# A two-block transformer kernel on one core: steps at the first block's end, at the start and around the GELUs in another order

## What is computed

```python
# first block, one layer
proj   = x @ w_in                               # q, k, v of three attentions, three gates
merged = sum(sigmoid(gate_i) * (attention_i @ w_branch_i) for i in range(3))
x      = layer_norm(ALPHA * x + merged @ w_out)
hidden = silu(x @ w_ffn_in[:, :2816]) * (x @ w_ffn_in[:, 2816:])
x      = layer_norm(ALPHA * x + hidden @ w_ffn_out)
# second block, one layer
q, k, v, u, vv = split(rms_norm(x) @ w_in_2)
attn   = attention(rope(rms_norm(q)), rope(rms_norm(k)), v)
sg     = gelu(u) * (sg_w @ rms_norm(gelu(vv)) + sg_b)      # the gated branch
x      = x + concat(rms_norm(attn), rms_norm(sg)) @ w_o_2
x      = x + (silu(conv(gate)) * conv(up)) @ w_down_2      # rms_norm and w_up_2 before the conv
```

## Time and profile before

| | |
|---|---|
| time before, median of 3 runs | 1495.82 us (1495.65 to 1495.94) |
| the profiled execution's own time | 1495.67 us |
| its span in the profile | 1494.2 us |
| PE busy | 1465.1 us, 98% of the span |
| DVE busy | 1003.1 us, 67% |
| ACT busy | 784.9 us, 53% |
| POOL busy | 64.1 us, 4% |
| chain that ended last | PE 82%, DVE 10%, ACT 4%, issue 2% |
| granted TensorE clock | 1.0 over the whole span |

### The profile page before, as it was taken

The page is one execution under the profiler, slowest core; times in us unless marked ns, Lnnn a source line. Parts: engine busy times, 40 slices in busy tenths (PEclk is TensorE's granted clock), DMA queues, the critical chain, the costliest instruction groups (busy, mean ns, idle before and its releaser), DMA issues.

```text
span 1494.2 us, 18393 instructions
## 1 busy us (share of the span) xinstructions
PE 1465.1 (98%) x7191; PEld 1203.8 (81%) x7191; DVE 1003.1 (67%) x1349; ACT 784.9 (53%) x1124; POOL 64.1 (4%) x100
## 2 busy tenths in 40 slices
PE   7999999999999999999999999999999999999998
PEld 5788887888887787887878887788888888888887
DVE  5656885864556655885865555877766668777765
ACT  3565644443443555745344333686655557756553
POOL 2000000000001000000010000210000012000000
PEclk9999999999999999999999999999999999999999
DMA  8544643575564535552765664436555644455551
GB/s 317 188 155 131 237 170 124 171 241 182 184 209 156 203 116 158 183 169 85 234 214 174 201 190 169 142 115 195 184 182 169 197 151 158 155 166 187 170 188 66
DMA packets 167317, 260.99 MB, mean 175 GB/s; under 512 B 8768, under 2 KB 106720, under 8 KB 166720
## 3 DMA queue, kind: packets, MB, share of 16 engines
q1 hardware_dynamic: 166048, 252.03, 51.6%
q0 software_dynamic: 896, 6.74, 1.2%
q10 hardware_dynamic: 288, 1.05, 0.2%
HBM read 258.74 MB, written 1.05 MB: 174 GB/s over the span
## 4 chain that ended last, share of the span: by engine, by line
PE 82%; DVE 10%; ACT 4%; issue 2%; POOL 1%; DMA 1%; SPq 0%; DVEq 0%; ACTq 0%
PE ps L384 15%; PE ps L388 15%; PE ps L386 15%; PE ps L457 10%; PE ps L459 9%; PE ps L458 9%; DVE wlo L1500 3%; ACT whi L1069 2%; PE ps L1001 1%; PE ps L511 1%; PE ps L534 1%; PE ps L414 1%; DVE x L1519 1%; DVE x L1517 1%; PE ps L524 1%
## 5 line engine op out<-in xcount | busy, mean ns | idle before, releaser
L1500 DVE TENSOR_TENSOR wlo<-raw,whi 128x2048 fp32r<-128x2048 f32 (+1 forms) x238 | 528.2, 2229 | 275.0 <-ACT whi L1069 274.4
L1069 ACT ACTIVATE whi<-raw 128x2048 fp32r<-128x2048 f32 (+1 forms) x238 | 441.7, 1865 | 204.7 <-PE ps L388 124.9
L384 PE MATMUL ps<-whi,xTh 128*128 128x512 f32 x704 | 277.4, 394 | 0.0
L388 PE MATMUL ps<-whi,xTl 128*128 128x512 f32 x704 | 274.4, 390 | 0.0
L386 PE MATMUL ps<-wlo,xTh 128*128 128x512 f32 x704 | 274.1, 389 | 0.0
L457 PE MATMUL ps<-whi,xTh 128*128 128x512 f32 (+3 forms) x640 | 251.1, 392 | 7.4 <-DVE xTl L1538 3.4
L459 PE MATMUL ps<-whi,xTl 128*128 128x512 f32 (+3 forms) x640 | 242.1, 378 | 0.0
L458 PE MATMUL ps<-wlo,xTh 128*128 128x512 f32 (+3 forms) x640 | 241.4, 377 | 0.0
L388 PEld LDWEIGHTS ps<-whi,xTl 128*128 128x128 f32 x704 | 132.1, 188 | 27.9
L384 PEld LDWEIGHTS ps<-whi,xTh 128*128 128x128 f32 x704 | 132.2, 188 | 27.6 <-issue 0.8
L386 PEld LDWEIGHTS ps<-wlo,xTh 128*128 128x128 f32 x704 | 132.3, 188 | 26.4
(11 more groups left out here) (185 smaller groups left out, 1635.2 us busy)
## 6 DMA issues: line engine op xcount, KB each, us to landing
raw<-in_w_in SPq DMA_DIRECT2D x124, 512.0 KB, 4.6
raw<-in_w_ffn_in SPq DMA_DIRECT2D x88, 512.0 KB, 4.8
raw<-in_w_up SPq DMA_DIRECT2D x88, 512.0 KB, 4.9
raw<-in_w_ffn_out SPq DMA_DIRECT2D x44, 512.0 KB, 4.4
raw<-in_w_down SPq DMA_DIRECT2D x44, 512.0 KB, 4.6
raw<-in_w_branch SPq DMA_DIRECT2D x24, 512.0 KB, 4.6
raw<-in_w_out SPq DMA_DIRECT2D x16, 512.0 KB, 4.5
raw<-in_w_o SPq DMA_DIRECT2D x16, 512.0 KB, 4.5
```

What stands on the lines that cost most here:

```text
L384: PE.matmul(o, ah, hi[:, j, b], start=first and kt == 0, stop=False)
L388: mm = PE.matmul(o, al, hi[:, j, b], start=False, stop=last and j == c - 1 and i == len(kts) - 1)
L1069: AC.activation(m.whi[:, i % SPLIT, 0:w], m.raw[:, slot, 0:w], ACT.Copy).then_inc(s.w_hi, 1)
L1500: DV.tensor_tensor(m.wlo[:, i % SPLIT, 0:w], m.raw[:, slot, 0:w], m.whi[:, i % SPLIT, 0:w].bitcast(F32), ALU.subtract).then_inc(s.w_lo, 1)
```

## The change

1. Start: half 0 of x is loaded in two parts, the second on ACT's queue ahead of the layer norm's two vectors; x's half 1 is loaded behind the second weight piece instead of between the two.
2. End of the first block, both layers, on DVE: `add_down(0)` and `stats(0)` go ahead of the subtraction of piece `later`; centring and scaling are separate steps, with `hidden_half(1)` between them; the split of the second quarter and of one more weight piece go ahead of `add_down(1)`. (`later` is the number of the next layer's first piece.)
3. There on PE: the first quarter of x is transposed ahead of the last `down` step's products, not in their middle.
4. Second block: DVE counts up after each of a quarter's four remainders, and PE waits per 128 columns (`remainders=4`). At the end of its first layer the second quarter of x is transposed behind the last products. `conv_turn` stands one column block later (three matmuls).
5. First attention: in group 4, ACT's rounding of one piece goes behind both copies of transposed weights.
6. Gated branch: the one-element GELU is gone, and the GELUs of `u` stand behind group 2's exponentials, not ahead of them.

```diff
@@ sync_program
-    SP.dma_start(m.x[:, 0, :], t["x"][0, 0:P, :]).then_inc(s.x_in, 16)
+    SP.dma_start(m.x[:, 0, 0:512], t["x"][0, 0:P, 0:512]).then_inc(s.x_in, 16)
...
         load_piece(w1[:, 0:4, 0:512], 4, 512)
+        load_piece(w1[:, 4:8, 0:512], 4, 512)
         if not L:
             SP.dma_start(m.x[:, 1, :], t["x"][0, P:S, :]).then_inc(s.x_in2, 16)
-        load_piece(w1[:, 4:8, 0:512], 4, 512)
@@ tensor_program
     def x_ready(th, kt):
-        if kt in (0, 4):
-            PE.wait_ge(s.turn_lo, x_lo[th, kt // 4])
+        count, remainders = x_lo[th, kt // 4]
+        if remainders == 4:
+            PE.wait_ge(s.turn_lo, count - 3 + kt % 4)
+        elif kt in (0, 4):
+            PE.wait_ge(s.turn_lo, count)
...
         def first_x_turn(th, kt):
-            if kt == 1:
-                turn_x(0, 0)
+            if kt == 0:
+                turn_x(0, 0, remainders=last_use)
...
         def down_turn(th, kt):
             if kt == 1:
-                for n4 in range(2):
-                    turn_x(0, n4)
+                turn_x(0, 0, remainders=4)
...
         def first_conv_turn(th, kt):
-            if (th, kt) == (0, 2):
+            if (th, kt) == (0, 3):
                 bank_free(2)
                 conv_turn()
...
+        if L + 1 < DEPTH:
+            turn_x(0, 1, remainders=4)
@@ scalar_program
+    AC.dma_start(m.x[:, 0, 512:D], t["x"][0, 0:P, 512:D]).then_inc(s.x_in1, 16)
     AC.dma_start(m.vec[:, 0:D], t["ln_g"][0:1, :].broadcast_to([P, D])).then_inc(s.vec, 16)
...
-            catch(1, L, "na", g, 2, ahead=SPLIT - (g == 4))
+            catch(1, L, "na", g, 2, ahead=0 if g == 4 else SPLIT)
...
-            if g == 2:
-                AC.activation(m.small[:, 60:61], m.half[:, 0:1], ACT.Gelu_apprx_tanh)
...
-            catch(2, L, "at", g, 1, ahead=0)
+            if g != 2:
+                catch(2, L, "at", g, 1, ahead=0)
...
+            if g == 2:
+                catch(2, L, "at", 2, 1, ahead=0)
@@ vector_program
         hidden_half(0)
         h_lo(slice(0, P), 2)
-        split_to(later + 1)
         add_down(0, (1, L, "dn", NSTEP - 1))
-        hidden_half(1)
         for n4 in range(2):
             stats(0, n4)
+        split_to(later + 1)
+        DV.wait_ge(s.vec, 32 * (L + 2))
+        center(0, 0)
+        hidden_half(1)
+        scale_up(0, 0)
         h_lo(slice(P, S), 2)
-        DV.wait_ge(s.vec, 32 * (L + 2))
-        apply(0)
+        center(0, 1)
+        scale_up(0, 1)
...
         split_to(later + 2)
-        add_down(1, (1, L, "dn", NSTEP - 1))
         if L + 1 < DEPTH:
             turn_lo_quarter(0, 1)
         else:
             turn_lo_gains(0, 1, 16)
+        split_to(later + 3)
+        add_down(1, (1, L, "dn", NSTEP - 1))
         for n4 in range(2):
             stats(1, n4)
-        split_to(later + 3 + (L + 1 < DEPTH))
+        if L + 1 < DEPTH:
+            split_to(later + 4)
         apply(1)
```

More of the change, by code:

```diff
@@ L408, in gate_cols, with turn_quarter @@
         return m.gate[:, th, kt * P:(kt + 1) * P]
-    def turn_quarter(src, th, n4):
+    def turn_quarter(src, th, n4, remainders=1):
         bank = ps[:, 4 + 2 * th + n4, :].rearrange("p (k s) -> p k s", k=4)
@@ L415, in turn_quarter, with turn_x @@
         mm.then_inc(s.turned, 1)
-        return n.up("turn_lo")
-    def turn_x(th, n4, ready=None):
+        return n.up("turn_lo", remainders)
+    def turn_x(th, n4, ready=None, remainders=1):
         if ready:
@@ L424, in turn_x @@
             PE.wait_ge(s.normed, n.up("normed"))
-        x_lo[th, n4] = turn_quarter(x_cols, th, n4)
+        x_lo[th, n4] = turn_quarter(x_cols, th, n4, remainders), remainders
     def x_ready(th, kt):
-        if kt in (0, 4):
-            PE.wait_ge(s.turn_lo, x_lo[th, kt // 4])
+        count, remainders = x_lo[th, kt // 4]
[3 more added lines that the diff above has]
+            PE.wait_ge(s.turn_lo, count)
     x_lo = {}
@@ L840, in tensor_program @@
         up(end, (1,), (1,))
+        last_use = 1 if L + 1 < DEPTH else 4
         def last_half_turn(th, kt):
@@ L852, in tensor_program @@
         down(end, (1,), first_x_turn)
-        turn_x(0, 1)
+        turn_x(0, 1, remainders=last_use)
     for L in range(DEPTH):
@@ L858, in x_ready_turn @@
             if kt in ((1, 2), (5, 6))[L == 0]:
-                turn_x(1, kt - (1, 5)[L == 0])
+                turn_x(1, kt - (1, 5)[L == 0], remainders=4)
         for i, (name, kts, width, th, before) in enumerate((("q", (4, 4), 512, 0, x_ready), ("k", (8,), 256, 0, x_ready_turn),
@@ L1510, in stats, with center, scale_up, apply @@
             DV.bn_aggr(m.mv[:, th, :], m.bn[:, th, :, :].rearrange("p a b -> p (a b)")).then_inc(s.moments, 1)
-    def apply(th, n4s=(0, 1)):
-        if 0 in n4s:
+    def center(th, n4):
+        if n4 == 0:
             DV.wait_ge(s.rstd, n.up("rstd"))
[L1515 to L1521, removed]
+        c = slice(n4 * 512, n4 * 512 + 512)
+        then(DV.scalar_tensor_tensor(out=m.x[:, th, c], in0=m.x[:, th, c], scalar=m.mv[:, th, 0:1], in1=m.vec[:, c],
+                                     op0=ALU.subtract, op1=ALU.mult))
+    def scale_up(th, n4):
+        c = slice(n4 * 512, n4 * 512 + 512)
+        DV.scalar_tensor_tensor(out=m.x[:, th, c], in0=m.x[:, th, c], scalar=m.small[:, th:th + 1],
+                                in1=m.vec[:, D + n4 * 512:D + n4 * 512 + 512], op0=ALU.mult,
+                                op1=ALU.add).then_inc(s.normed, 1)
+    def apply(th):
+        for n4 in range(2):
+            center(th, n4)
+            scale_up(th, n4)
     def turn_lo_quarter(th, n4, scale=1.0):
@@ L1537, in turn_lo_gains @@
             o = slice(th * P, (th + 1) * P)
[L1538 to L1541, removed]
+            DV.scalar_tensor_tensor(out=m.xTl[:, kt, o], in0=ps[:, 4 + 2 * th + n4, kt % 4 * P:(kt % 4 + 1) * P],
+                                    scalar=m.pcol[:, col + kt:col + kt + 1], in1=m.xTh[:, kt, o].bitcast(F32), op0=ALU.mult,
+                                    op1=ALU.subtract).then_inc(s.turn_lo, 1)
     def wait_sum(name, th):
@@ L1742, in vector_program @@
     DV.wait_ge(s.x_in, 16)
-    for n4 in range(2):
-        stats(0, n4)
+    stats(0, 0)
+    DV.wait_ge(s.x_in1, 16)
+    stats(0, 1)
     for L in range(DEPTH):
```

6 lines of the change are left out of this document (3 added, 3 removed).

## The result

| | before | changed |
|---|---|---|
| median of 4 runs | 1495.80 us (1495.65 to 1495.94) | 1510.45 us (1508.02 to 1511.09) |
| span of the profiled execution | 1494.2 us | 1508.8 us |
| mean granted clock | 1.0 | 0.993 |

The ratio is 1.0095, with a 95% interval of 1.0083 to 1.0107: slower by 14.65 us. That is the direction that was forecast, but more than twice the size, and above the range (1496.9 to 1505.2). The page of the changed kernel shows none of this in its shares: PE is busy for 98%, as in the earlier trace rows.

A forecast was written before the change was run, and what follows sets the result against it. PE bounds the kernel, busy for 98% of the span. Terms 6.2 + 2.6 - 1.4 - 0.95 - 0.3 - 0.2 = +5.95 on 1495.67 led to 1501.7 us; range 1496.9 to 1505.2, the forecast's own 1499.8 to 1503.6.

The forecast's parts named there:

- gated branch: Both layers: second `sg_mix` waits 2.3 us for the later GELU, weights' transposes come late; +3.1 per layer, +6.2.
- first block's ends: DVE's new order makes hidden transposes 3.2 us late, partly recovered; +1.55 first layer, +1.05 second, +2.6 together.
- conv: Three matmuls fill PE's 0.72 us wait for ACT's eviction; -0.7 in each layer, -1.4.
- seam: Between the second block's layers: moved transposes fill the 0.80 us wait for all four remainders; -0.95.
- start: Second weight piece lands earlier, the norm's vectors later; -0.3, bounds -0.6 and +1.0.
- the rest: Per-column waits elsewhere -0.2; first attention's rounding, SP's loads and extra semaphore counts 0.
- rival (d): Clock falls in three new waits of some 3 us, PE's next products at 1.2 GHz; +2.8, 1504.5; chance 10%.
- second wait of about 3 us: Sign in the changed profile: PE waits about 3 us for x near the second layer's end.
- rival (e): Gated branch: both table loads drain and cost about as much again, +5.5: 1507; chance 3%.
- (a): First block's ends come out even or better, at the low bound -1.9; sum +1.45: 1497.1; chance 15%.
- (b): First block's ends: hidden products not late, all 8.3 us of waiting goes; sum -4.95: 1490.7; chance 8%.
- (c): Gated branch: PE isn't held by the bank, -1.0 instead of +6.2; sum -1.25: 1494.4; chance 6%.

The follow-up runs named there:

- gelu_only_busy: Kernel before with item 6 alone, plus group 2's sixteen products of weights and values done twice on PE inside the GELU wait: 1502.61 us.
- all_busy: Changed kernel with work of no use (doubled products, identity transposes) in all five long waits of PE: 1503.45 us.
- start_only: Kernel before with item 1 alone: 1495.08 us beside 1495.82.
- gelu_only: Kernel before with item 6 alone (gated branch): 1505.90 us beside 1495.68.
- conv_right: Change without items 2, 3 and 6, with the `conv_turn` inside the third step's up-projection one column block later: 1493.82 us beside 1493.73.
- first_part_kept: Changed kernel with item 6 undone and the first part of item 2 (piece, sum, hidden products, statistics) in the old order: 1496.60 us.

## Why the prediction was wrong

| term | forecast | measured | from |
|---|---|---|---|
| gated branch | +6.2 | +6.9 | gelu_only_busy |
| first block's ends | +2.6 | +2.4 | all_busy less the other rows |
| conv | -1.4 | -0.2 | starts of PE in ends_kept |
| seam | -0.95 | -0.6 | starts of PE in ends_kept |
| start | -0.3 | -0.7 | start_only |
| the rest | -0.2 | 0 | taken as nothing |
| sum without the clock | +5.95 | +7.8 | all_busy: +7.8 |
| clock | 0 | +7.0 | changed kernel less all_busy |

(The last two add up to 14.8, against 14.65: the times come from two occasions.)

**The step that failed** is the one the forecast left at nothing: rival (d), "The clock falls in the new waits", with a chance of 10% and an estimate of +2.8. It was not a rival to the forecast but a part of it, since the forecast itself predicted the waits. It happened, and it cost 7.0. Two things in its working were wrong. It counted three waits of some 3 us: the two for the hidden products and the "second wait of about 3 us" that the last part of the prediction names itself, at 948.53 with 2.76. There were five, for the two of 2.3 us in the gated branch, a term of the forecast's own sum, bring the clock down too. And it priced each at 0.9 us (2.8 / 3), with part of the slow work hidden in waits for DVE; measured are 7.0 / 5 = 1.4 each. A little was hidden: at 948.53 the slow work runs over a wait of 0.53 us for half 1 of x that all_busy has there, and that fall cost about 0.8. But behind all five PE was busy for 2.93 us or more of 3.00.

The prediction says that nothing in the trace of before shows what follows on 3 us of waiting, since its longest wait after the start is 1.5 us. That passes over the start itself. PE waits there for 8.60 us, and then:

```profile
8.60 2.18 PE L566 MATMUL ps<-ident 128*128 128x128 f32 x9 [8.60 <-DMA rope<-in_rope]
10.58 1.06 PE L414 MATMUL ps<-ident,x 128*128 128x128 f32 x4
...
932.07 0.60 PE L414 MATMUL ps<-ident,x 128*128 128x128 f32 x4
```

Four transposes of x take 1.06 us there and 0.60 later, the same two times as in the gated branch above, and this lasts to about 13.3 us. So the clock was not full over the whole span, although the column shows 1.0. It is a wait of another length, at a place where PE has done nothing yet, so it does not tell that 2.3 us are enough; but it has the price at hand, some 4.7 us of work at half speed, and with it both ends should have been kept in the sum. With the lengths known now, five stretches of 3.0 us at half speed lose 1.5 us each, 7.5 in all, and 1501.7 + 7.5 = 1509.2 lies within 1.3 of the result. That nearness is in part luck: the terms without the clock were 1.8 too low, and the stretches were of 3 to 6 us with something hidden in them. The Trainium skill, "TensorE: Matmul & The Clock Gate", section HAM oscillation, says that a kernel which alternates bursts of matmuls with waits runs the bursts at half clock; the windows of the changed kernel agree, with 0.50 to 0.57 behind each wait, and gelu_only's second layer, at 1.00 behind 2.31 us, does not. I cited it and gave it 10%, where it should have been in the sum.

**Gated branch: right in mechanism, close in size.** `sg_mix` waited 2.30 us, as worked out. The rest of the layer added 1.15 at full clock, where I had 0.8: in gelu_only's second layer 3.5 in all, against 3.1. No drain beside the table loads was seen: the GELU starts 0.01 us after the load ends (993.62 + 1.28 = 994.90, start 994.91), the load starts 0.02 us after ACT's last instruction, and the load for group 3 (1002.84 + 1.28 = 1004.12, first exponential at 1004.13) is no different. So rival (e) did not occur.

**The first block's ends: right.** The hidden transposes came 3.3 us late by place, the forecast said 3.2; the chain through piece, POOL's 2.12 and the centring ran as laid out. The size without the clock is 2.4 against 2.6; it is worked out as all_busy's 7.8 less the other rows (7.8 - 6.9 + 0.7 + 0.2 + 0.6), so it carries their errors, and the equality of the two sums is no check of its own. Read directly from PE's starts in all_busy, it is 1.35 in the first layer and 0.75 in the second, 2.1 in all, where the forecast had 1.55 and 1.05.

**Conv: wrong place, and wrong theory.** The step "PE waited 0.72 us for ACT's eviction; three matmuls of 0.23 now stand in that gap" took the row of one `conv_turn` for another. The kernel calls it from several places with one line number, and the change moves only the first. The wait that the earlier trace rows shows under the name of the first `conv_turn` is that of the second, inside the third step's up-projections: it is the one that conv_right's edit moved. Even there it would have been worth less than 0.1 a layer (conv_right).

**Seam.** The wait went, as forecast. Of the 0.95, 0.6 came out. By PE's starts in the changed kernel 0.8 is won at the place itself, and 0.35 is lost again 6 us later, at 1229.57, where PE comes 0.1 us after the end of a weight piece's subtraction on DVE (1227.18 + 2.28 = 1229.46); before, that piece was done 1.3 us ahead of PE. These rows fit a PE that now runs up to DVE's piece; no run tested it.

**Rivals (a), (b), (c)** did not occur. The range was too narrow above: it held (d) at 1504.5 and little more. Without the clock the kernel stands at 1503.45, inside the forecast's own range, with misses of both signs in it: the gated branch and the conv were 0.7 and 1.2 dearer than forecast, the start 0.4 better.

The best of the versions run is ends_kept, the change without items 2, 3 and 6, at 1493.73: 2.0 us or 0.13% under the kernel before.

## What to carry to other kernels

When a forecast contains waits of TensorE longer than any in the trace at hand, the clock's half level belongs in the sum: take the work that follows each at twice its length for the 3 to 6 us seen here, and both ends into the range. To see such a stretch, read the lengths of like instructions too, and not the clock column alone. Where such a wait can't be removed, matmuls of no use inside it can pay (7.0 us here with five waits); not making the wait pays more. When work is reordered on an engine that is the pace of a stretch, as DVE at the block's end and, by PE's waits, ACT in the conv, the wait moves and little is won; and before a row is set against an edit, the call it belongs to has to be found, since a helper's line stands for all of its calls.

## What was not expected of the hardware

The same wait of 2.31 us was followed by a clock of 0.59 in one layer and by 1.00 in the other, in one execution. Over the traces: in the changed kernel all five waits of 2.30 to 3.42 were followed by 0.50 to 0.57; in first_part_kept waits of 2.26 and 2.28 by 0.58 and 0.63, and one of 2.60 by 1.00. So at this length it is open from one wait to the next, and such a kernel's times spread: 3 us over four runs of the changed kernel (mean clock 0.993 in three, 0.995 in the fastest), against 0.3 over four of the kernel before and 0.4 over four of all_busy. And identity transposes, 128 columns wide, were enough to hold the clock (28 of them in the 3.4 us at the first layer's end of all_busy, at 1.00).
